# A two-block transformer kernel at 256 tokens: index scores over 128 rows, the start reordered, the final norm split, tensors moved by 64 bytes

## The chip, the cores and the metric

The kernel runs on one core of a Trainium2 chip. The metric is device time in microseconds (us), lower is better. TensorE (PE) multiplies; its weight loads (PEld) overlap its matmuls. VectorE (DVE), ScalarE (ACT), GpSimd (POOL) and SyncE (SP) are the other engines; SP issues nearly all transfers.

## The reference

`x` is 256 rows of 2048, all in float32. Two layers of a first block (an attention with index scores, then a block attention), one layer of a second block (a gated delta net beside a compressed attention, then a gated feed-forward of width 5632), and a last norm. What matters for the change:

```python
# layer a: index scores
qi = rope(qi.reshape(B, T, IDX_HEADS, IDX_DIM), pos)      # 16 heads of 64
ki = rope(ki.reshape(B, T, 1, IDX_DIM), pos)[:, :, 0]     # one key of 64
rel = relu(einsum('bqhd,bsd->bqhs', qib, ki) * IDX_DIM ** -0.5)
score = einsum('bqh,bqhs->bqs', wib, rel)
_, sel = lax.top_k(score, n_keep)                          # 64 of 256 keys
...
# the feed-forward, and the final norm
x = x + (silu(h2 @ w_ffn_gate) * (h2 @ w_ffn_up)) @ w_ffn_down
return x * lax.rsqrt(mean(x * x, axis=-1) + NORM_EPS) * norm_f_w
```

## The kernel before

Every product with weights runs in "chunks" of 512 output columns (`weight_plan`). A chunk is a row of "quads": a quad is 4 x 128 rows of the weight (1 MB), landed in one of four buffers `W`. Float32 is split into a rounded high part and a rest: ScalarE writes `WH` (`round_up`), VectorE the rest `WL` (`rest`, L1673), each in two halves of 128x1024, and TensorE adds three matmuls, WH with XH, WL with XH, WH with XL (L795, L796, L797), each 128x128 times 128x512. The activations stand turned, as XH and XL; for the last product of the feed-forward they are HH and HL. A half quad is two "visits", one for each 128 rows of x, of six matmuls each. The sums stand in two banks ACC, which ScalarE or VectorE empties at the end of a chunk (`take`).

All other work (norms, attention, delta net, turning x) is written as generators, started at a fixed visit by `side_plan` on every engine and advanced one step at each visit (`sides_of`). So each engine's order is fixed by program order, and semaphores join them. TensorE's side steps thus lie between two groups of six main matmuls.

The places of the change:

- Start. `turn("x.a", c)` turns slice c (512 columns) of x: TensorE transposes four 128x128 tiles into bank TP0 and four into TP1 (L428), ScalarE writes XH with the norm's gain (L818, two of 128x256 for each bank), VectorE XL (L1198, L1199). Slices 0 and 1 are turned ahead of the loop over the chunks; 2 and 3 are side tasks at visits 2 and 6. In the prologue ScalarE and VectorE do for n = 0 and 1: the whole of slice n, then both halves of quad n's weights. SP issues slice, quad, slice, quad in turn (L386, L399).
- ScalarE's helper `A` loads a table before Exp or Ln if another is held (L814); another load is put at L818 where an activation needs one. The roots of the first norm are taken at visit 11; `take` of the first chunk scales by them.
- Index scores (`index` on three engines). After rotation VectorE copies the one key of 64 twice, side by side, into KI (L1337, L1338), so that its transpose KIT holds the key in partitions 0 to 63 and again in 64 to 127. QIT holds two heads above each other. For head h TensorE multiplies the 64 partitions of its half, in two matmuls (L525, L526) of 128 and 256 columns, one head a visit; ScalarE takes relu, VectorE adds it into SCORE (L1354), and then, in eight rounds of `max` and `match_replace`, finds the 64 largest. The attention's scores have the same two shapes over 128 partitions (L464, L465).
- Addresses. Tensors are laid one after another. `root_steps` has 100 columns; behind it come the arena (all scratch), SG, H, HH, HL and the final gain.
- End. Squares of each slice of the last x are summed by ScalarE (`squares("f", c)`), slices 0 to 2 as side tasks in the last chunks, slice 3 after the loop. `roots` takes the mean, Ln, Exp and one refinement on VectorE. Then VectorE scales each 128 rows of 2048 by root and gain in one pass (L1703), and SP stores them (L403).

```python
    for n in range(2):                       # act_program; dve_program alike, with rest
        for _ in turn("x.a", n):
            pass
        for half in range(2):
            round_up(n, half)
...
    for t in range(TB):                      # dve_program, its end
        STT(M.X[:, t, :], M.X[:, t, :], M.rs[:, 4, t:t + 1], M.NF, ALU.mult, ALU.mult).then_inc(*did("normalised", t))
```

## Time and profile before

| | before |
|---|---|
| median of 3 runs | 2363.6 us (2363.17 to 2369.43) |
| the profiled execution | 2363.92 us, of which the span 2362.6 |
| TensorE matmuls busy | 2322.3 us, 98% of the span |
| VectorE busy | 1367.0 us, 58% |
| ScalarE busy | 1158.6 us, 49% |
| mean granted TensorE clock | 0.997 |
| read from HBM | 396.23 MB, 169 GB/s over the span |

The span runs from the first to the last instruction of the profiled execution; its own time is 1.3 us more. The busy share of TensorE is of the instructions as recorded, which overlap: a main matmul lasts 0.39 us, and the next starts 0.23 us after it. So its speed is read from starts.

### The profile page before, as it was taken

The numbers are of one execution on the slowest core, as the hardware profiler recorded it, in microseconds if no ns is written. First come the engines' busy times: TensorE is split into PE (matmuls) and PEld (weight loads), VectorE is DVE, ScalarE is ACT, GpSimd is POOL, SyncE is SP. The second block draws the span as 40 slices with busy tenths as digits, with TensorE's granted clock in tenths as the row PEclk, the third lists the DMA queues.
The fourth block names the chain that finished last, engine by engine and source line by source line (L and its number), as shares of the span: only waits on it lengthen the run. The fifth ranks groups of instructions, "written<-read, shape, count | busy, mean of one in ns | idle before, by whom it ended". The sixth has DMA issues, their size and how long they took to land.

```text
span 2362.6 us, 27386 instructions
## 1 busy us (share of the span) xinstructions
PE 2322.3 (98%) x11188; PEld 1921.5 (81%) x11188; DVE 1367.0 (58%) x1930; ACT 1158.6 (49%) x1635; POOL 9.6 (0%) x17
## 2 busy tenths in 40 slices
PE   8999999999999999999999999999999999999997
PEld 6788788888788888888888887888888888888886
DVE  5676555656555577687666555645545544544554
ACT  5456654556654564453445455445444344434443
POOL 0000000000000000000000000000000000000000
PEclk9999999999999999999999999999999999999999
DMA  7454445564545553333554455555565565555552
GB/s 260 132 177 153 143 154 188 174 196 143 162 159 196 161 166 107 125 126 107 166 191 143 157 164 178 178 196 193 181 195 181 194 192 184 194 184 191 195 179 107
DMA packets 204269, 400.10 MB, mean 169 GB/s; under 512 B 12656, under 2 KB 12816, under 8 KB 203760
## 3 DMA queue, kind: packets, MB, share of 16 engines
q1 hardware_dynamic: 201920, 391.08, 50.3%
q0 software_dynamic: 1648, 6.32, 1.0%
q8 instruction: 89, 1.46, 0.3%
q10 hardware_dynamic: 576, 0.95, 0.1%
q14 instruction: 36, 0.29, 0.0%
HBM read 396.23 MB, written 2.10 MB: 169 GB/s over the span
## 4 chain that ended last, share of the span: by engine, by line
PE 93%; DVE 3%; ACT 2%; issue 1%; DMA 0%; SPq 0%; DVEq 0%; ACTq 0%
PE ACC L795 28%; PE ACC L797 27%; PE ACC L796 27%; PE TP L428 2%; ACT arena L818 1%; PE PV L629 1%; PE SC L624 1%; DVE WL L1673 1%; PE PV L632 1%; PE SC L465 1%; PE TP L473 1%; PE SC L675 1%; PE PV L483 0%; PE PV L482 0%; PE PV L481 0%
## 5 line engine op out<-in xcount | busy, mean ns | idle before, releaser
L1673 DVE TENSOR_TENSOR WL<-W,WH 128x1024 fp32r<-128x1024 f32 x740 | 900.8, 1219 | 656.0 <-ACT WH L818 654.3
L818 ACT ACTIVATE WH<-W 128x1024 fp32r<-128x1024 f32 x740 | 781.3, 1056 | 839.6 <-PE ACC L797 835.3
L795 PE MATMUL ACC<-WH,XH 128*128 128x512 f32 x2592 | 1045.7, 403 | 7.0 <-ACT arena L818 4.8
L797 PE MATMUL ACC<-WH,XL 128*128 128x512 f32 x2592 | 1013.5, 391 | 0.0
L796 PE MATMUL ACC<-WL,XH 128*128 128x512 f32 x2592 | 1011.7, 390 | 0.0
L795 PEld LDWEIGHTS ACC<-WH,XH 128*128 128x128 f32 x2592 | 488.1, 188 | 116.8 <-issue 15.2
L797 PEld LDWEIGHTS ACC<-WH,XL 128*128 128x128 f32 x2592 | 487.4, 188 | 105.9
L796 PEld LDWEIGHTS ACC<-WL,XH 128*128 128x128 f32 x2592 | 488.7, 189 | 92.1 <-issue 1.0
L795 PE MATMUL ACC<-WH,HH 128*128 128x512 f32 x352 | 139.3, 396 | 0.0
L797 PE MATMUL ACC<-WH,HL 128*128 128x512 f32 x352 | 137.8, 392 | 0.0
L796 PE MATMUL ACC<-WL,HH 128*128 128x512 f32 x352 | 137.6, 391 | 0.0
L818 ACT ACTIVATE arena<-ACC,reciprocal_roots 128x512 f32<-128x512 f32 x86 | 58.9, 688 | 44.3 <-PE ACC L797 44.0
L795 PEld LDWEIGHTS ACC<-WH,HH 128*128 128x128 f32 x352 | 66.1, 188 | 16.6 <-DVE X L1667 1.8
L797 PEld LDWEIGHTS ACC<-WH,HL 128*128 128x128 f32 x352 | 66.1, 188 | 14.9
L796 PEld LDWEIGHTS ACC<-WL,HH 128*128 128x128 f32 x352 | 66.2, 188 | 13.7
L818 ACT ACTIVATE arena<-SC 128x256 f32<-128x256 f32 (+2 forms) x70 | 27.1, 391 | 90.8 <-PE SC L624 65.1
L818 ACT ACTIVATE arena<-TP 128x384 f32<-128x384 f32 (+2 forms) x91 | 46.2, 510 | 42.4 <-PE TP L473 21.6
L1667 DVE TENSOR_TENSOR X<-ACC,X 128x512 f32<-128x512 f32 x48 | 33.0, 687 | 43.7 <-PE ACC L797 43.7
L818 ACT ACTIVATE arena<-arena,maxima 128x128 f32<-128x128 f32 x96 | 42.6, 446 | 15.0 <-DVE maxima L1299 14.9
L1196 DVE TENSOR_TENSOR XL<-TP,XH 128x512 fp32r<-128x512 f32 x32 | 22.1, 691 | 38.5 <-ACT XH L818 38.5
L818 ACT ACTIVATE arena<-arena 128x512 f32<-128x512 f32 (+4 forms) x50 | 37.0, 756 | 12.2 <-DVE arena L1419 9.6
L1511 DVE TENSOR_TENSOR arena<-arena,PV 128x256 f32<-128x256 f32 x48 | 20.2, 421 | 34.2 <-PE PV L632 23.0
(255 smaller groups left out, 1414.2 us busy)
## 6 DMA issues: line engine op xcount, KB each, us to landing
W<-in_w_in SPq DMA_DIRECT2D x84, 1024.0 KB, 4.9
W<-in_a_w_in SPq DMA_DIRECT2D x48, 1024.0 KB, 5.1
W<-in_w_ffn_gate SPq DMA_DIRECT2D x44, 1024.0 KB, 5.2
W<-in_w_ffn_up SPq DMA_DIRECT2D x44, 1024.0 KB, 5.2
W<-in_w_ffn_down SPq DMA_DIRECT2D x44, 1024.0 KB, 5.1
W<-in_b_w_in SPq DMA_DIRECT2D x40, 1024.0 KB, 5.1
W<-in_a_w_out SPq DMA_DIRECT2D x16, 1024.0 KB, 5.0
W<-in_b_w_out SPq DMA_DIRECT2D x16, 1024.0 KB, 5.1
```

The source lines that it names most:

```text
L428: ins = TR(TP[j][:, (2 * k + t) * P:(2 * k + t + 1) * P], src(c)[:, t, col:col + P], ident)
L465: MM(SC[b][:, P:3 * P], QT[:, i, P:T], kt(0, T), start=True, stop=True).then_inc(*did("scores_multiplied", l, g, i))
L473: ins = TR(TP[b][:, s * P:(s + 1) * P], M_PR(l)[b][:, s * P:(s + 1) * P], ident)
L624: ins = MM(sc[:, h * P:(h + 1) * P], m["M"][:, h, :], m["S"][:, h, :], start=True, stop=True)
L629: ins = MM(pv[:, h * P:(h + 1) * P], m["TI"][:, h, :], m["Y"][:, h, :], start=True, stop=True)
L632: ins = MM(pv[:, (PH + h) * P:(PH + h + 1) * P], m["Y"][:, h, :], m["TI"][:, h, :], start=True, stop=True)
L795: MM(out, hx, WH[:, k, 0:ch.width], start=q == 0 and k == 0, stop=False)
L796: MM(out, hx, WL[:, k, 0:ch.width], start=False, stop=False)
L797: ins = MM(out, lx, WH[:, k, 0:ch.width], start=False, stop=last and k == QK - 1)
L818: return nc.scalar.activation(out, in_, func, **how)
L1667: ins = TT(x, acc, x, ALU.add)
L1673: TT(tiles_of(M.WL[n % 2], ch, half), tiles_of(M.W[n % 4], ch, half), tiles_of(M.WH[n % 2], ch, half).bitcast(F32), ALU.subtract).then_inc ...
```

## The change

Five things, all in one edit:

1. KI and KIT become two of each: one holds the key in partitions 0 to 63 and zeros above, the other zeros and the key. Head h multiplies all 128 partitions of QIT, which hold two heads, with the KIT that has zeros for the other head. Both are placed elsewhere in the arena.
2. Of slice 1 of x, TensorE's transposes move into the loop, as a side task at visits 0 and 1. ScalarE and VectorE alternate in the prologue: half a slice, half a quad.
3. The table for Ln and Exp is loaded at ScalarE's start, and for the final norm ahead of the squares of slice 0.
4. Slices 0 to 2 of the last x are multiplied by the final gain as side tasks (`gained`), three visits after each is ready. The scaling by the root is shared: ScalarE takes the left 1024 columns and stores them from its own queue, VectorE the right 1024 (the last 512 with their gain), stored by SP.
5. `root_steps` gets 116 columns, which moves all that lies behind it by 64 bytes: arena, SG, H, HH, HL and the final gain began 64 bytes past a multiple of 128, and now begin on one.

```diff
+    begin(0, "second_turn")
     for c in range(2, NC_D):
         begin(4 * c - 6, "turn", "x.a", c)
...
         begin(after(f"d.p2c{c}"), "squares", "f", c)
+        begin(after(f"d.p2c{c}") + 3, "gained", c)
...
-    M.dn_norms, roots = sb("delta_norms", [P, 2, 8]), sb("root_steps", [P, 100])
+    M.dn_norms, roots = sb("delta_norms", [P, 2, 8]), sb("root_steps", [P, 116])
...
-    M.KW, M.KI, M.WI, M.KIT, M.TOP = cut(18944, TB, ID + IH), cut(19104, TB, 2 * ID), cut(19360, TB, IH), cut(19392, T), cut(19648, TB, 8)
+    M.KW, M.KI, M.WI, M.KIT, M.TOP = cut(18944, TB, ID + IH), cut(21200, TB, 2, 2 * ID), cut(19360, TB, IH), cut(21712, 2, T), cut(19648, TB, 8)
...
-        sp.dma_start(K.out[0, t * P:(t + 1) * P, :], M.X[:, t, :]).then_inc(*did("x_stored", t, by=16))
+        sp.dma_start(K.out[0, t * P:(t + 1) * P, 2 * CH:], M.X[:, t, 2 * CH:]).then_inc(*did("x_stored", t, by=16))
...
+    sp.wait_ge(*at("x_stored_left", TB - 1))
...
-        for t in range(TB):
-            ins = TR(TP[0][:, t * P:(t + 1) * P], M.KI[:, t, :], ident)
+        for odd in range(2):
+            for t in range(TB):
+                ins = TR(TP[0][:, (odd * TB + t) * P:(odd * TB + t + 1) * P], M.KI[:, t, odd, :], ident)
...
-            MM(banks[b][:, 0:P], M.QIT[half, h // 2, 0:P], M.KIT[half, 0:P], start=True, stop=True)
-            MM(banks[b][:, P:3 * P], M.QIT[half, h // 2, P:T], M.KIT[half, :], start=True, stop=True).then_inc(*did("index_scored", h))
+            MM(banks[b][:, 0:P], M.QIT[:, h // 2, 0:P], M.KIT[:, h % 2, 0:P], start=True, stop=True)
+            MM(banks[b][:, P:3 * P], M.QIT[:, h // 2, P:T], M.KIT[:, h % 2, :], start=True, stop=True).then_inc(*did("index_scored", h))
...
-    for c in range(2):
-        for _ in turn("x.a", c):
-            pass
+    for _ in turn("x.a", 0):
+        pass
+
+    def second_turn():
+        yield from turn("x.a", 1)
...
+        if l == "f" and c == 0:
+            act.preload_act_table_set("natural_log_exp_and_others")
+            held[0] = "log_exp"
...
+    act.preload_act_table_set("natural_log_exp_and_others")
+    held[0] = "log_exp"
     act.wait_ge(*at("gains_landed"))
     for n in range(2):
-        for _ in turn("x.a", n):
-            pass
-        for half in range(2):
+        for half, _ in enumerate(turn("x.a", n)):
             round_up(n, half)
...
+    act.wait_ge(*at("gained", 1))
+    act.wait_ge(*at("reciprocal_roots", "f"))
+    for t in range(TB):
+        x = M.X[:, t, 0:2 * CH]
+        A(x, x, ACT.Copy, scale=M.rs[:, 4, t:t + 1]).then_inc(*did("normalised_left", t))
+        act.wait_ge(*at("normalised_left", t))
+        act.dma_start(K.out[0, t * P:(t + 1) * P, 0:2 * CH], x).then_inc(*did("x_stored_left", t, by=16))
...
-        V.tensor_copy(M.KI[:, :, 0:ID], M.KW[:, :, 0:ID])
-        V.tensor_copy(M.KI[:, :, ID:2 * ID], M.KW[:, :, 0:ID])
+        for odd in range(2):
+            V.tensor_copy(M.KI[:, :, odd, odd * ID:(odd + 1) * ID], M.KW[:, :, 0:ID])
+            V.memset(M.KI[:, :, odd, (1 - odd) * ID:(2 - odd) * ID], 0.0)
...
+    def gained(c):
+
+        dve.wait_ge(*at("final_gain_landed"))
+        dve.wait_ge(*at("squares_summed", "f", c))
+        x = M.X[:, :, c * CH:(c + 1) * CH]
+        TT(x, x, M.NF[:, c * CH:(c + 1) * CH].unsqueeze(1).to_broadcast([P, TB, CH]), ALU.mult).then_inc(*did("gained", c))
+        yield
...
-        STT(M.X[:, t, :], M.X[:, t, :], M.rs[:, 4, t:t + 1], M.NF, ALU.mult, ALU.mult).then_inc(*did("normalised", t))
+        x, y = (M.X[:, t, c * CH:(c + 1) * CH] for c in (2, 3))
+        STT(y, y, M.rs[:, 4, t:t + 1], M.NF[:, 3 * CH:], ALU.mult, ALU.mult)
+        TS(x, x, M.rs[:, 4, t:t + 1], None, ALU.mult).then_inc(*did("normalised", t))
```

How instructions move, at three places. ScalarE at the start, before: a table load, the whole slice, then both halves of the quad.

```order
L1154 DMA gains<-in_norm_gains 128x64
L818 ACT_TABLE_LOAD
L818 ACTIVATE XH<-TP,gains 128x256 x4
L818 ACTIVATE WH<-W 128x1024 x2
L818 ACTIVATE XH<-TP,gains 128x256 x4
L818 ACTIVATE WH<-W 128x1024 x2
```

And now (lines are shifted by the edit, L818 is L825):

```order
L1164 DMA gains<-in_norm_gains 128x64
L1165 ACT_TABLE_LOAD
L825 ACTIVATE XH<-TP,gains 128x256 x2
L825 ACTIVATE WH<-W 128x1024
L825 ACTIVATE XH<-TP,gains 128x256 x2
L825 ACTIVATE WH<-W 128x1024
```

The first rounding of weights moved ahead of the second half of the slice, and the load of the table no longer follows a wait for a transpose.

TensorE at the start, before (16 transposes, then the main matmuls):

```order
L428 MATMUL TP<-consts,X 128x128 x16
L795 MATMUL ACC<-WH,XH 128x512
L796 MATMUL ACC<-WL,XH 128x512
L797 MATMUL ACC<-WH,XL 128x512
L795 MATMUL ACC<-WH,XH 128x512
```

And now (L428 is L431, L795 to L797 are L802 to L804):

```order
L431 MATMUL TP<-consts,X 128x128 x8
L802 MATMUL ACC<-WH,XH 128x512
L803 MATMUL ACC<-WL,XH 128x512
L804 MATMUL ACC<-WH,XL 128x512
L802 MATMUL ACC<-WH,XH 128x512
L803 MATMUL ACC<-WL,XH 128x512
L804 MATMUL ACC<-WH,XL 128x512
L431 MATMUL TP<-consts,X 128x128 x4
```

Eight transposes, those of slice 1, moved behind the first and (the other four) the second six main matmuls.

VectorE at the end, before:

```order
L1667 TENSOR_TENSOR X<-ACC,X 128x512 x2
L1207 TENSOR_REDUCE root_steps<-sums_of_squares 128x2
L1209 TENSOR_SCALAR root_steps<-root_steps 128x2
L1231 TENSOR_TENSOR root_steps<-reciprocal_roots 128x2
L1233 SCALAR_TENSOR_TENSOR root_steps<-root_steps 128x2
L1235 SCALAR_TENSOR_TENSOR reciprocal_roots<-root_steps,reciprocal_roots 128x2
L1703 SCALAR_TENSOR_TENSOR X<-X,reciprocal_roots,final_gain 128x2048 x2
```

And now, where L1672 is the gain of one slice, done between the roundings of the last weights:

```order
L1672 TENSOR_TENSOR X<-X,final_gain 128x2x512
L1700 TENSOR_TENSOR WL<-W,WH 128x1024
L1694 TENSOR_TENSOR X<-ACC,X 128x512 x2
L1224 TENSOR_REDUCE root_steps<-sums_of_squares 128x2
L1226 TENSOR_SCALAR root_steps<-root_steps 128x2
L1248 TENSOR_TENSOR root_steps<-reciprocal_roots 128x2
L1250 SCALAR_TENSOR_TENSOR root_steps<-root_steps 128x2
L1252 SCALAR_TENSOR_TENSOR reciprocal_roots<-root_steps,reciprocal_roots 128x2
L1729 SCALAR_TENSOR_TENSOR X<-X,reciprocal_roots,final_gain 128x512
L1730 TENSOR_SCALAR X<-X,reciprocal_roots 128x512
L1729 SCALAR_TENSOR_TENSOR X<-X,reciprocal_roots,final_gain 128x512
L1730 TENSOR_SCALAR X<-X,reciprocal_roots 128x512
```

Of the two passes of 2048 columns behind the roots, four of 512 are left on VectorE.

## Rows read from the trace of the kernel before

**Rows 1.** The page, part 4: chain that ended last, by engine
```profile
PE 93%; DVE 3%; ACT 2%; issue 1%; DMA 0%; SPq 0%; DVEq 0%; ACTq 0%
```
**Rows 2.** Timeline of the start: start us, us, engine, line, operation, [idle before <-releaser]
```profile
1.23 0.48 SPq L399 DMA_DIRECT2D W<-in_a_w_in  x1
...
5.54 1.94 PE L428 MATMUL TP<-consts,X 128*128 128x128 f32 x8 [5.54 <-DMA X<-in_x]
6.71 1.28 ACT L818 ACT_TABLE_LOAD   x1 [6.71 <-PE TP L428]
...
9.45 2.02 ACT L818 ACTIVATE WH<-W 128x1024 fp32r<-128x1024 f32 x2
...
11.83 0.79 PE L795 MATMUL ACC<-WH,XH 128*128 128x512 f32 x1
...
14.98 0.56 PE L796 MATMUL ACC<-WL,XH 128*128 128x512 f32 x1
```
**Rows 3.** The transfer issued at 1.23: KB, us from issue to landing
```profile
W<-in_a_w_in SPq DMA_DIRECT2D x1, 1024.0 KB, 7.2
```
**Rows 4.** Timeline of the end of the first chunk
```profile
34.98 1.28 ACT L814 ACT_TABLE_LOAD   x1 [0.52 <-DVE root_steps L1209]
...
38.51 1.25 ACT L818 ACTIVATE arena<-ACC,reciprocal_roots 128x512 f32<-128x512 f32 x2
...
39.32 0.47 PE L795 MATMUL ACC<-WH,XH 128*128 128x512 f32 x1 [1.91 <-ACT arena L818]
```
**Rows 5.** Timeline, TensorE around one index score
```profile
83.31 0.40 PE L797 MATMUL ACC<-WH,XL 128*128 128x512 f32 x1
...
83.64 0.29 PEld L525 LDWEIGHTS SC<-arena 64*128 64x128 f32 x2 [0.36 <-issue]
...
84.49 0.19 PEld L795 LDWEIGHTS ACC<-WH,XH 128*128 128x128 f32 x1 [0.33 <-issue]
```
**Rows 6.** Timeline, TensorE around one score of the attention
```profile
168.16 0.39 PE L797 MATMUL ACC<-WH,XL 128*128 128x512 f32 x1
...
168.85 0.58 PE L795 MATMUL ACC<-WH,XH 128*128 128x512 f32 x1
```
**Rows 7.** Timeline ahead of the first index transpose
```profile
74.13 0.18 DVE L1339 TENSOR_SCALAR arena<-arena 128x32 f32<-128x32 f32 x1
...
74.39 0.59 PEld L509 LDWEIGHTS TP<-consts,arena 128*128 128x128 f32 x4
```
**Rows 8.** Windows: us, busy (x instructions) of PE, PEld, DVE, ACT, POOL, clock, DMA, GB/s
```profile
102.20:121.70 19.50, 19.50 (x84) 12.59 (x83) 16.72 (x30) 8.93 (x15) 0.00 (x0) 1.00 0.33 108
122.00:145.00 23.00, 23.00 (x104) 18.82 (x104) 22.52 (x62) 10.63 (x12) 0.00 (x0) 1.00 0.46 145
```
**Rows 9.** Timeline, TensorE's wait behind the choice of the largest
```profile
139.78 0.19 PEld L795 LDWEIGHTS ACC<-WH,XH 128*128 128x128 f32 x1 [0.29 <-DVE WL L1673]
```
**Rows 10.** Timeline, first and last of 179 matmuls with XH, of 65 with HH
```profile
1708.30 0.39 PE L796 MATMUL ACC<-WL,XH 128*128 128x512 f32 x1
...
1748.67 0.39 PE L797 MATMUL ACC<-WH,XL 128*128 128x512 f32 x1
...
2334.33 0.40 PE L796 MATMUL ACC<-WL,HH 128*128 128x512 f32 x1
...
2348.99 0.39 PE L797 MATMUL ACC<-WH,HL 128*128 128x512 f32 x1
```
**Rows 11.** Windows of these two stretches
```profile
2334.30:2349.00 14.70, 14.70 (x66) 12.02 (x64) 4.05 (x4) 3.16 (x7) 0.00 (x0) 1.00 0.01 1
1708.30:1748.70 40.40, 40.40 (x180) 33.41 (x178) 19.98 (x18) 17.64 (x18) 0.00 (x0) 1.00 0.61 195
```
**Rows 12.** Timeline of the end
```profile
2351.39 1.28 ACT L814 ACT_TABLE_LOAD   x1 [0.52 <-DVE root_steps L1209]
...
2353.82 4.61 DVE L1703 SCALAR_TENSOR_TENSOR X<-X,reciprocal_roots,final_gain 128x2048 f32<-128x2048 f32 x2
2356.20 2.62 SPq L403 DMA_DIRECT2D out<-X  x2
```

More of the change, by code:

```diff
@@ L521, in index @@
         for h in range(IH):
-            b, half = h % 4, slice(ID * (h % 2), ID * (h % 2 + 1))
+            b = h % 4
             name = ("SC0", "SC1", "PV0", "PV1")[b]
             wait_empty(name)
-            MM(banks[b][:, 0:P], M.QIT[half, h // 2, 0:P], M.KIT[half, 0:P], start=True, stop=True)
-            MM(banks[b][:, P:3 * P], M.QIT[half, h // 2, P:T], M.KIT[half, :], start=True, stop=True).then_inc(*did("index_scored", h))
+            MM(banks[b][:, 0:P], M.QIT[:, h // 2, 0:P], M.KIT[:, h % 2, 0:P], start=True, stop=True)
+            MM(banks[b][:, P:3 * P], M.QIT[:, h // 2, P:T], M.KIT[:, h % 2, :], start=True, stop=True).then_inc(*did("index_scored", h))
             emptied[name] = ("index_taken", h)
@@ L758, in narrow @@
         yield
-    tasks["narrow"] = narrow
+    tasks["narrow"], tasks["second_turn"] = narrow, second_turn
     live, visit, taken = [], 0, [None] * TB
@@ L925, in index @@
         act.wait_ge(*at("index_transposed", 4))
-        A(M.KIT, TP[0][:, 0:T], ACT.Copy).then_inc(*did("index_turned", 4))
+        A(M.KIT.rearrange("p n t -> p (n t)"), TP[0][:, :], ACT.Copy).then_inc(*did("index_turned", 4))
         yield
@@ L1676, in dve_program @@
                  dn_gates=dn_gates, dn_conv=dn_conv, dn_norms=dn_norms, dn=dn, dn_out=dn_out, nsa_rope=nsa_rope, compress=compress, compressed=compressed,
-                 nsa_queries=nsa_queries, nsa_attend=nsa_attend, mixed=mixed)
+                 nsa_queries=nsa_queries, nsa_attend=nsa_attend, mixed=mixed, gained=gained)
     dve.wait_ge(*at("gains_landed"))
     for n in range(2):
-        for _ in turn("x.a", n):
-            pass
-        for half in range(2):
+        for half, _ in enumerate(turn("x.a", n)):
             rest(n, half)
@@ L1699, in dve_program @@
         pass
-    dve.wait_ge(*at("final_gain_landed"))
+    dve.wait_ge(*at("gained", 2))
     dve.wait_ge(*at("reciprocal_roots", "f"))
     for t in range(TB):
-        STT(M.X[:, t, :], M.X[:, t, :], M.rs[:, 4, t:t + 1], M.NF, ALU.mult, ALU.mult).then_inc(*did("normalised", t))
+        x, y = (M.X[:, t, c * CH:(c + 1) * CH] for c in (2, 3))
+        STT(y, y, M.rs[:, 4, t:t + 1], M.NF[:, 3 * CH:], ALU.mult, ALU.mult)
+        TS(x, x, M.rs[:, 4, t:t + 1], None, ALU.mult).then_inc(*did("normalised", t))
 def pool_program(K):
```

## The prediction

> **What bounds the kernel.** I read first the chain of waits: 93% of it is TensorE's own work [rows 1]. So what the change saves on TensorE, or where TensorE stands still, is saved in full; work taken from the other engines is worth nothing unless TensorE, or the end, waits for it. Then, in this order: the start and the end instruction by instruction, where TensorE is not yet, or no longer, the bound; the stretch of the index scores, for what lies between two main matmuls; then the steady pace of the matmuls by operand.
>
> About 0.3% (7.1 us) is what a measurement of this kernel can tell from no change.
>
> **The start.** TensorE turns slice 0 at 5.54, and ScalarE, woken by it, first loads a table (6.71 to 7.99), then writes four XH pieces and rounds the first weights from 9.45; 2.38 us later, at 11.83, the first weight matmul starts [rows 2]. The weights themselves were issued at 1.23 [rows 2] and took 7.2 us [rows 3]: they were there at 8.43. In the new order the table is loaded before any wait (1.28 us gone) and the first rounding stands behind two XH pieces instead of four; the four pieces fill 7.99 to 9.45, 0.37 each, so two are done near 7.5 and the rounding starts when the weights land, 8.43. That moves TensorE's start by 9.45 - 8.43 = 1.0 earlier, to 10.8.
> Against it: the eight transposes of slice 1 stood ahead of that matmul, while TensorE had nothing else; now four follow each of the first two groups of six matmuls. Eight take 1.94 [rows 2] at the lower clock (1.2 GHz, which is what a matmul start every 0.45 from 11.83 to 14.98 is, eight starts, seven intervals [rows 2]; steady it is 0.227, below). If all eight run at the low level, TensorE is 1.94 - 1.0 = 0.9 behind; if the second four come after the rise, they cost half and it is 0.5 behind; if the rise follows the earlier start, it is even. I take 0.3 behind, ends -1.0 and +0.9.
> At the end of the first product TensorE stands idle for 1.91, until 39.32, while ScalarE empties the accumulator (from 38.51). In ScalarE's unbroken work ahead of that is a table load at 34.98 of 1.28 [rows 4], which is gone: the table from the start serves Ln and Exp too. So 38.51 - 1.28 + 0.3 = 37.53, and with the same 0.81 from emptying to matmul TensorE goes on at 38.34: **-1.0**. TensorE itself is free at 39.32 - 1.91 + 0.3 = 37.7, so ScalarE still decides. Ends: -2.3 and -0.4.
>
> **The index scores.** There are 16 visits, each with products of 128 and of 256 columns over 64 rows between two groups of main matmuls. From the start of the last main matmul to that of the next, 83.31 to 84.49, is 1.18, with two holes in weight loading that nothing explains, 0.36 and 0.33, at the change to the 64-row form and back [rows 5]. A product of the same columns over 128 rows, the scores of the attention, takes 168.16 to 168.85 = 0.69 [rows 6], with no hole. The new scores have just this form: 16 x 0.49 = **-7.8**. The zeros cost no column. Two more transposes of the key: at 1.94 / 8 at the low clock, half of that at the high, +0.2. VectorE clears two half blocks more ahead of the first index transpose; its last small step there takes 0.18 and ends at 74.31, and TensorE's weight load starts at 74.39 [rows 7]; so of two such steps, overlapping a little, some 0.3, 0.2 shows: **+0.2**. ScalarE's copy of 512 instead of 256 columns lies behind six main matmuls (1.4 us).
> What is late next is VectorE. From its first step for one score to that for the eighth after it (102.2 to 121.7) it is busy 16.72 of 19.50 us, 2.8 free [rows 8]; eight shorter visits take away 8 x 0.49 = 3.9. It falls at least 1.1 behind; since it must still idle a little at the first of them I take 1.4. Behind it comes the choice of the largest 64, in which it is busy 22.52 of 23.0 [rows 8], and at 139.78 TensorE already waits 0.29 for VectorE's WL [rows 9]. So nothing of the lag is made up before that wait, and it comes out as **+1.4** there. Ends: 0 (later work has slack) and +3.9 (all of those eight visits).
>
> **The operand at 128 bytes.** Sixteen more columns in the table of root steps move the arena, SG, H, HH and HL by 64 bytes, from 64 beyond a multiple of 128 to a multiple; X, XH, XL and the weights already lie on one. In two stretches without side work the matmuls with XH take (1748.67 - 1708.30) / 178 = 0.2268, those with HH (2348.99 - 2334.33) / 64 = 0.2291 [rows 10]. Other work is not what slows HH: in its stretch 1 GB/s is moved and VectorE and ScalarE are nearly idle, in that of XH 195 GB/s [rows 11]. There are 1,056 HH or HL matmuls: 1,056 x 0.0023 = **-2.4**, if the address is the reason; the only other difference is which tensor. Ends: -2.4 and 0. The attention's products read the arena but are paced by their passes, so I give them nothing.
>
> **The end.** After the last square, ScalarE loads a table (2351.39, 1.28), VectorE starts scaling at 2353.82, and SyncE issues the first store at 2356.20, 2.38 later; the last byte is in 6.4 after that, at 2362.6 [rows 12]. The table is now loaded ahead of the final squares of slice 0, where ScalarE only waits for TensorE: -1.28. The gain is multiplied in ahead, after each of three slices, 1.2 us of VectorE while it idles between roundings. What stays is, per 128 rows, 512 + 512 columns on VectorE and 1024 on ScalarE, side by side. A 1024-column pass of ScalarE takes 1.0 (the pair of roundings at 9.45 takes 2.02) [rows 2] and VectorE's two passes at most half of the 2.3 of 2048 columns (4.61 for two) [rows 12], so the first stores go out about 1.1 after the start of scaling instead of 2.38: -1.27. The same 2.1 MB then leave in the same 6.4, as second stores follow 1.1 to 1.6 later, well before the first are out. Sum **-2.5**; ends -1.3 (store no earlier) and -3.2.
> The Trainium skill (ScalarE: Activation LUTs, What ACT_TABLE_LOAD costs) adds a drain of 1.38 us to every load; by it the two loads on the path would give 2.8 more and the kernel 2348.9. Here such a drain finds no room: from the last load's end, 2352.67, to the scaling at 2353.82 are 1.15, and Ln, Exp and three steps of VectorE lie in them. The trace bears out the 1.28 alone.
>
> **Sum.** -1.0 - 7.8 + 0.2 + 0.2 + 1.4 - 2.4 - 2.5 = -11.9. The profiled execution took 2363.92 for a span of 2362.6; its time becomes 2352.0. The median of the runs shown is 0.3 lower, so I predict **2351.7**.
>
> **Rivals.**
> (a) The address is not why HH is slower (its data, or its being written by another path). All else holds: 2354.1. For it: no row compares one tensor at two addresses. Against it: XH and HH have the same shape and writers.
> (b) VectorE keeps more: the full 3.9. Then 2354.2. For it: 22.52 of 23.0 busy. Against: VectorE's own 2.8 free in that stretch.
> (c) The padded scores do not do what they say: the holes belong to the alternation of these two shapes, not to 64 rows. Then -7.8 and +1.4 both go: 2358.1, no change by the bound. Against it: [rows 6] alternates the same two shapes in the same place without a hole.
> (d) A load holds ScalarE longer than its row: the idle 0.52 ahead of the one at 34.98, put down to VectorE, is the load's own, and so at the end. Then 1.0 more goes: 2350.7. Against it: both stand right behind a step of VectorE that Ln needs anyway. (The Trainium skill's drain, above, would be the larger form of this.)
> (e) Slower: TensorE's clock. The change leaves TensorE idle from 7.5 to 10.8 and then mixes short transposes into the first matmuls. Each microsecond longer at 1.2 GHz costs 1 - 0.227 / 0.45 = 0.5. It takes 24 us more at the low level to use up the 11.9, and about 38 to be 0.3% slower, 2371. For it: [rows 2] shows the low level at this place. Against it: there it was over within 3.5 us of steady matmuls.
> Each stall that is moved may also gain or lose such a stretch, at 0.5 per microsecond 1 to 2 us either way.
>
> **Chances.** Forecast 0.64, own range 2349 to 2355; (a) 0.12; (b) 0.08; (c) 0.07; (d) 0.04; (e) 0.02; several small ones failing together, near 2357, 0.03. Faster by over 0.3% (below 2356.5) are the forecast, (a), (b) and (d): 0.88. Within: (c) and the last, 0.10. Slower: 0.02. The range for 8 in 10 takes in (a), (b), (d) and the ends of the unknown costs: 2347.5 to 2357.0.
>
> **What would show it.** Right: 0.69 between the main matmuls around each score, no hole; HH's pace 0.2268; one table load fewer ahead of 40 us and none after the last matmul; the first store 4.7 us after the start of the last matmul, where it is 2356.20 - 2348.99 = 7.2 now; TensorE waiting 1.5 us on WL shortly after the index stretch, where it now waits 0.3. Wrong, and with it the number: visits still near 1.18; HH still 0.2291; a longer stretch of the low clock at the start; a wait for the stores' second halves.

## The result, and the profile after

The changed kernel takes 2352.48 us, median of five runs (2351.88 to 2353.9), against 2363.6 for five runs of the kernel before (2360.28 to 2369.82): a ratio of 0.9937, 95% interval 0.9916 to 0.9959. Predicted were 2351.7 and faster. The profiled execution took 2353.76 for a span of 2352.4; its prediction was 2352.0.

| | after |
|---|---|
| span of the profiled execution | 2352.4 us (-10.2) |
| TensorE matmuls busy | 2313.6 us, 98% |
| VectorE, ScalarE busy | 1368.8, 1159.8 us |
| mean granted TensorE clock | 0.997 |

The page's chain of waits says the same as [rows 1]:

```profile
PE 92%; DVE 4%; ACT 2%; issue 1%; DMA 0%; ACTq 0%; SPq 0%; DVEq 0%
```

The busy sums tell nothing of where 10 us went. What tells it is the start of each of the 8,832 main matmuls, which stand in the same order in both kernels. The table sets before and after side by side, numbered from 0.

| main matmul | before | after | difference | what lies in between |
|---|---|---|---|---|
| 0 | 11.83 | 10.57 | -1.26 | the start |
| 24 | 19.87 | 20.31 | +0.44 | eight transposes in the loop |
| 96 | 39.32 | 38.47 | -0.85 | no table load ahead of the first emptying |
| 246 | 82.08 | 81.40 | -0.68 | two more key transposes, +0.22 |
| 342 | 121.50 | 114.45 | -7.05 | 16 index scores, -6.37 |
| 420 | 139.78 | 133.80 | -5.98 | the wait for WL, +1.07 |
| 6432 | 1792.32 | 1786.21 | -6.11 | nothing that stays: no single place moves it by more than 0.4 |
| 8831, the last | 2348.99 | 2341.09 | -7.90 | HH, -1.8 |
| end of the span | 2362.6 | 2352.4 | -10.2 | the end, -2.3 |

Both profiles hold the same two short stretches at a granted clock of 0.50, 3.4 us each (from 264.5 and 1165.6 before, from 258.1 and 1159.2 after), so this table sets like beside like.

The start, in the timeline of the changed kernel, which answers to [rows 2]:

```profile
1.74 1.28 ACT L1165 ACT_TABLE_LOAD   x1 [1.74 <-issue]
...
6.78 0.84 ACT L825 ACTIVATE XH<-TP,gains 128x256 fp32r<-128x256 f32 x2 [3.75 <-DMA gains<-in_norm_gains]
...
8.21 1.06 ACT L825 ACTIVATE WH<-W 128x1024 fp32r<-128x1024 f32 x1 [0.58 <-DMA W<-in_a_w_in]
...
9.29 1.22 DVE L1700 TENSOR_TENSOR WL<-W,WH 128x1024 fp32r<-128x1024 f32 x1 [0.69 <-ACT WH L825]
...
10.57 0.80 PE L802 MATMUL ACC<-WH,XH 128*128 128x512 f32 x1 [3.18 <-DVE WL L1700]
```

The table is in before anything is waited for, and ScalarE then waits 0.58 for the weights: the rounding cannot start earlier than 8.21, as predicted (8.43). The first matmul is released by VectorE's WL. The end of the first chunk, which answers to [rows 4]:

```profile
35.42 0.20 ACT L825 ACTIVATE reciprocal_roots<-root_steps 128x2 f32<-128x2 f32 x1 [0.53 <-DVE root_steps L1226]
...
37.66 1.24 ACT L825 ACTIVATE arena<-ACC,reciprocal_roots 128x512 f32<-128x512 f32 x2
...
38.47 0.47 PE L802 MATMUL ACC<-WH,XH 128*128 128x512 f32 x1 [0.63 <-ACT arena L825]
```

TensorE's idle time went from 1.91 to 0.63. The 0.53 ahead of the root stays although no load follows it: it was never the load's. One index score, in the timeline of TensorE:

```profile
84.68 0.40 PE L804 MATMUL ACC<-WH,XL 128*128 128x512 f32 x1
84.91 0.38 PE L529 MATMUL SC<-arena 128*128 128x128 f32 x2
85.13 0.60 PE L530 MATMUL SC<-arena 128*128 128x256 f32 x2
85.38 0.58 PE L802 MATMUL ACC<-WH,XH 128*128 128x512 f32 x1
85.79 0.39 PE L803 MATMUL ACC<-WL,XH 128*128 128x512 f32 x1
```

From main to main it is 0.70, as the attention's [rows 6], and no weight load waits. But look one matmul further: 85.38 to 85.79 is 0.41. In the kernel before, behind the hole, it is less:

```profile
84.49 0.50 PE L795 MATMUL ACC<-WH,XH 128*128 128x512 f32 x1
84.82 0.39 PE L796 MATMUL ACC<-WL,XH 128*128 128x512 f32 x1
```

That is 0.33. So from the last main matmul ahead of the score to the second one behind it, a score takes from 83.31 to 84.82 = 1.51 before and 84.68 to 85.79 = 1.11 now: 0.40, not 0.49. Then the wait for the weights' low parts, which answers to [rows 9]:

```profile
132.53 1.22 DVE L1700 TENSOR_TENSOR WL<-W,WH 128x1024 fp32r<-128x1024 f32 x1
...
133.79 0.19 PEld L802 LDWEIGHTS ACC<-WH,XH 128*128 128x128 f32 x1 [1.29 <-DVE WL L1700]
133.80 0.50 PE L802 MATMUL ACC<-WH,XH 128*128 128x512 f32 x1 [0.87 <-DVE WL L1700]
```

An undisturbed stretch with HH, first and last of 65, which answers to [rows 10]:

```profile
2326.56 0.40 PE L803 MATMUL ACC<-WL,HH 128*128 128x512 f32 x1
...
2341.09 0.39 PE L804 MATMUL ACC<-WH,HL 128*128 128x512 f32 x1
```

14.53 for 64 intervals is 0.2270 each (before 0.2291). And the end, which answers to [rows 12]:

```profile
2343.50 0.20 ACT L825 ACTIVATE reciprocal_roots<-root_steps 128x2 f32<-128x2 f32 x1 [0.54 <-DVE root_steps L1226]
...
2344.62 1.15 ACT L825 ACTIVATE X<-X,reciprocal_roots 128x1024 f32<-128x1024 f32 x1 [0.68 <-DVE reciprocal_roots L1252]
2344.64 0.75 DVE L1729 SCALAR_TENSOR_TENSOR X<-X,reciprocal_roots,final_gain 128x512 f32<-128x512 f32 x1
2345.31 0.48 DVE L1730 TENSOR_SCALAR X<-X,reciprocal_roots 128x512 f32<-128x512 f32 x1
...
2345.80 0.37 ACTq L1197 DMA_DIRECT2D out<-X  x1
2345.82 1.42 SPq L405 DMA_DIRECT2D out<-X  x2
```

No table load; ScalarE and VectorE are done within 0.02 of each other, and the first store is issued 4.71 after the last matmul's start (before 7.2).

### The profile page after: what moved, and what is told of

It reads as the page before. It is cut to its first block, busy times and chain, and to the rows that moved or that the text cites. A ratio compares the mean times of both kernels' runs of the same rounds, so it can differ in the third digit from the quotient of the medians.

```text
span 2352.4 us, 27404 instructions
## 1 busy us (share of the span) xinstructions
PE 2313.6 (98%) x11190; PEld 1923.8 (82%) x11190; DVE 1368.8 (58%) x1937; ACT 1159.8 (49%) x1636; POOL 9.6 (0%) x17
## 4 chain that ended last, share of the span: by engine, by line
PE 92%; DVE 4%; ACT 2%; issue 1%; DMA 0%; ACTq 0%; SPq 0%; DVEq 0%
PE ACC L802 27%; PE ACC L804 27%; PE ACC L803 27%; PE TP L431 2%; ACT arena L825 1%; DVE WL L1700 1%; PE PV L633 1%; PE SC L628 1%; PE PV L636 1%; PE SC L468 1%; PE TP L476 1%; PE SC L679 1%; PE PV L485 0%; PE PV L486 0%; PE PV L484 0%
## 5 line engine op out<-in xcount | busy, mean ns | idle before, releaser
L825 ACT ACTIVATE WH<-W 128x1024 fp32r<-128x1024 f32 x740 | 781.4, 1056 | 835.8 <-PE ACC L804 832.8
L802 PE MATMUL ACC<-WH,XH 128*128 128x512 f32 x2592 | 1046.9, 404 | 9.8 <-DVE WL L1700 4.0
L804 PE MATMUL ACC<-WH,XL 128*128 128x512 f32 x2592 | 1013.5, 391 | 0.0
L802 PEld LDWEIGHTS ACC<-WH,XH 128*128 128x128 f32 x2592 | 488.4, 188 | 115.0 <-issue 9.0
L804 PEld LDWEIGHTS ACC<-WH,XL 128*128 128x128 f32 x2592 | 487.2, 188 | 105.2
L802 PE MATMUL ACC<-WH,HH 128*128 128x512 f32 x352 | 138.6, 394 | 0.0
L804 PE MATMUL ACC<-WH,HL 128*128 128x512 f32 x352 | 137.1, 389 | 0.0
L825 ACT ACTIVATE arena<-ACC,reciprocal_roots 128x512 f32<-128x512 f32 x86 | 58.9, 689 | 44.1 <-PE ACC L804 43.8
L802 PEld LDWEIGHTS ACC<-WH,HH 128*128 128x128 f32 x352 | 66.1, 188 | 16.5 <-DVE X L1694 2.0
L804 PEld LDWEIGHTS ACC<-WH,HL 128*128 128x128 f32 x352 | 66.1, 188 | 14.0
L825 ACT ACTIVATE arena<-SC 128x256 f32<-128x256 f32 (+2 forms) x70 | 27.1, 390 | 88.2 <-PE SC L628 65.4
L825 ACT ACTIVATE arena<-TP 128x384 f32<-128x384 f32 (+2 forms) x91 | 46.4, 513 | 42.6 <-PE TP L476 21.4
L825 ACT ACTIVATE arena<-arena,maxima 128x128 f32<-128x128 f32 x96 | 42.7, 447 | 15.0 <-DVE maxima L1316 14.9
L825 ACT ACTIVATE arena<-arena 128x512 f32<-128x512 f32 (+4 forms) x50 | 37.1, 756 | 12.2 <-DVE arena L1438 9.7
L825 ACT ACTIVATE XH<-TP,gains 128x256 fp32r<-128x256 f32 x64 | 26.8, 470 | 27.1 <-PE TP L431 23.3
```

The costliest lines, as they stand in the source:

```text
L802: MM(out, hx, WH[:, k, 0:ch.width], start=q == 0 and k == 0, stop=False)
L804: ins = MM(out, lx, WH[:, k, 0:ch.width], start=False, stop=last and k == QK - 1)
L825: return nc.scalar.activation(out, in_, func, **how)
```

## The experiments

Twelve kernels, each built from the one before or the changed one.

### The operand's address: the shift alone, and each operand by itself

Of the two operands of a main matmul the expectations call the 128x128 of activations (XH, XL, HH, HL) the stationary one and the 128x512 of weights (WH, WL) the moving one. `shift_only` is the kernel before with `root_steps` at 116 columns, nothing else. The other three move one operand:

```diff
-    M.dn_norms, roots = sb("delta_norms", [P, 2, 8]), sb("root_steps", [P, 100])      # shift_only
+    M.dn_norms, roots = sb("delta_norms", [P, 2, 8]), sb("root_steps", [P, 116])
...
+    sb("gap_ahead_of_hh", [P, 16])      # hh_only: HH, HL at 0 mod 128, the arena still at 64
...
+    sb("gap_ahead_of_xh", [P, 16])      # xh_64: XH, XL at 64 mod 128; a gap behind them restores the rest
...
+    sb("gap_ahead_of_wh", [P, 16])      # wh_64: WH, WL at 64 mod 128; a gap behind them restores the rest
```

> The kernel before, with root_steps of 116 columns: arena, SG, H, HH, HL and the gain all move from 64 off to a multiple of 128. Theory: HH's pace 0.2269, 2.3 us less, and the arena's products are paced by their passes and keep their times (an attention score 0.69 between main matmuls, the delta net's eight products 1.05): 2361.3. Rival (the arena's stationary operands gain too): those groups get shorter by 2 ns for each product and the time falls 2 to 4 us further.

> The kernel before, with 64 bytes of unused columns ahead of HH: HH, HL and the final gain lie on multiples of 128 bytes, arena, SG and H stay 64 off. Theory (the address of the stationary operand sets the pace): the 1,056 matmuls with HH go from one every 0.2291 us to one every 0.2269, 2.3 us in all, and nothing else moves. Rival (a) (HH's data or its writers): the pace stays 0.2291 and the time at 2363.6. A third reading, that the arena or H must move too, also leaves 0.2291.

> The kernel before, with 64 bytes of unused columns ahead of XH and 64 more behind XL: only XH and XL are moved, to 64 bytes past a multiple of 128. Theory (address of the stationary operand): the 7,776 main matmuls with XH slow from 0.2269 to 0.2291, so 7,776 x 0.0022 = 17 us, less what hides in waits: about 2380. Rival (a) (it is something of HH as a tensor): XH keeps 0.2269 and the time 2363.6.

> The kernel before, with WH and WL alone moved to 64 bytes past a multiple of 128: the moving operand of all 8,832 main matmuls. Theory in its narrow form (only the stationary operand's address counts): both paces as before, 0.2269 with XH and 0.2291 with HH, time 2363.6. Rival in its wide form (any operand off 128 bytes costs): both 0.0022 slower, 19 us, about 2383.

Measured: `shift_only` 2359.57 us, `hh_only` 2369.68, `xh_64` 2383.85, `wh_64` 2373.53, the kernel before in the same job 2372.65. These totals are one run each and carry something else (below, the clock: its mean was 0.997 in `shift_only` and `wh_64`, 0.992 or 0.993 in the others), so the pace is what counts. `shift_only`, for one, is 1.7 under the 2361.3 expected because its profile has no stretch at 0.50 near 1165 us. Timeline of `wh_64`, first and last of 191 matmuls with XH and of 65 with HH:

```profile
1891.49 0.39 PE L798 MATMUL ACC<-WL,XH 128*128 128x512 f32 x1
...
1934.98 0.39 PE L799 MATMUL ACC<-WH,XL 128*128 128x512 f32 x1
...
2344.11 0.39 PE L798 MATMUL ACC<-WL,HH 128*128 128x512 f32 x1
...
2358.62 0.39 PE L799 MATMUL ACC<-WH,HL 128*128 128x512 f32 x1
```

43.49 / 190 = 0.2289 with XH, which stands on a multiple of 128; 14.51 / 64 = 0.2267 with HH, which does not, and nor do the weights. With XH at 64 and the weights at 0 (`xh_64`) XH too is slow, 190 intervals of 0.2290:

```profile
1900.73 0.40 PE L798 MATMUL ACC<-WL,XH 128*128 128x512 f32 x1
...
1944.24 0.39 PE L799 MATMUL ACC<-WH,XL 128*128 128x512 f32 x1
```

So what decides is neither operand's own alignment, but whether both begin at the same place within 128 bytes. My expectation of `wh_64` had no such case. Over all undisturbed stretches, in ns:

| weights mod 128 | activations mod 128 | start to start | kernels |
|---|---|---|---|
| 0 | 0 | 226.9 | XH in all but two; HH after, `hh_only`, `shift_only` |
| 0 | 64 | 229.0 | HH before; XH and HH in `xh_64` |
| 64 | 0 | 229.1 | XH in `wh_64` |
| 64 | 64 | 227.0 | HH in `wh_64` |
| 0 | 32 | 233.3 | HH in `hh_32` |

`hh_only` and `shift_only` have the same pace. In `shift_only`, which moves the arena too, no interval with attention or delta net work in it, of some 450 up to matmul 3900, changed by more than 0.07 us, and all of them together by 0.3: the arena's move gains next to nothing.

`hh_32` is the changed kernel with `root_steps` at 124 columns, so HH begins 32 past a multiple of 128.

> The changed kernel, with root_steps of 124 columns instead of 116: all behind it, HH among it, lies 32 bytes past a multiple of 128. Theory A (the operand must start on a multiple of 128): HH's pace is 0.2291 or slower again, 2.3 us more than the changed kernel. Theory B (multiples of 32 are enough except 64): 0.2269 and no difference. The index scores and the end keep their times in both.

```profile
2333.56 0.40 PE L803 MATMUL ACC<-WL,HH 128*128 128x512 f32 x1
...
2348.49 0.40 PE L804 MATMUL ACC<-WH,HL 128*128 128x512 f32 x1
```

14.93 / 64 = 0.2333 here and over all stretches; all HH matmuls together take 5.75 us more than in the changed kernel, and the run took 2361.14. A quarter of 128 bytes off costs more than a half.

### The start and the end, each alone

`turn_only`: the kernel before with the second slice's transposes in the loop and half-and-half prologues. `table_only`: with the early load alone. `end_only`: with part 4 and the load ahead of the last squares.

```diff
+    act.preload_act_table_set("natural_log_exp_and_others")      # table_only: these two lines
+    held[0] = "log_exp"
...
-        for _ in turn("x.a", n):                                  # turn_only: this and second_turn
-            pass
-        for half in range(2):
+        for half, _ in enumerate(turn("x.a", n)):
...
+        begin(after(f"d.p2c{c}") + 3, "gained", c)                # end_only: this, gained and the shared scaling
```

> The kernel before, with slice 1 turned behind the first weights (all three engines' orders of the start as in the changed kernel) but the tables loaded where they were. Theory: the first main matmul starts near 10.9 to 11.6 instead of 11.83 (the table load of 1.28 still stands ahead of XH, so the weights' rounding starts at 8.73, not 8.43), the 25th some 0.4 to 0.8 us later than before (19.87), because eight transposes now run in the stream, and the 97th at 39.32 + 0.4 to 0.8, since the table load at 35 us is still in ScalarE's chain: about 0.5 us slower than before. Rival (the turning order itself gains): the 97th starts before 39.32.

> The kernel before, with only the table for Ln and Exp loaded at ScalarE's start. Theory: the four XH pieces start at 6.7 instead of 8.0 and the weights' rounding at 8.43, so the first main matmul starts no later than the transposes of slice 1 end, near 11.9 (they wait for slice 1, which lands at 9.9): no gain there; the gain is at the 97th main matmul, 39.32 - 1.28 + 0, bounded by the emptying of the accumulator behind TensorE: 38.1. So 1.2 us less than before, all of it from the second table load. Rival (the reordered turning is what gains at the start): less than 0.5 us.

> The kernel before, with only the end changed: gain ahead, scaling and stores shared, and the table loaded ahead of the final squares. Theory: up to the last matmul nothing moves (within 0.2 us); first store 4.7 us after the last matmul's start instead of 7.2, end 11.3 after it instead of 13.6: 2.3 us less. Rival (work put into the last chunks on VectorE and ScalarE delays the last weights): the last matmul starts more than 0.3 us later than 2348.99.

Measured: `turn_only` 2374.27 us, `table_only` 2361.71, the kernel before in the same job 2363.06, one run each. The total of `turn_only` carries some 10 us of the clock (below), so the starts are compared. "Rise" is where the pace of the main matmuls doubles, from one every 0.43 us to one every 0.23; the last column is matmul 96 less half of the rise.

| | matmul 0 | matmul 24 | matmul 96 | rise | matmul 96, less half the rise |
|---|---|---|---|---|---|
| before | 11.83 | 19.87 | 39.32 | 15.3 | 31.7 |
| `turn_only` | 11.07 | 20.70 | 40.13 | 16.1 | 32.1 |
| `table_only` | 11.46 | 19.89 | 38.06 | 15.9 | 30.1 |
| after | 10.57 | 20.31 | 38.47 | 15.8 | 30.6 |

The early table gives -1.26 at matmul 96. The new order of turning gives an earlier first matmul and then loses it: +0.8 alone, +0.4 beside the early table. But the rise moves from kernel to kernel without a cause in the code: among the eight kernels whose start is that of the kernel before it lies between 13.8 and 16.0, and matmul 96 between 38.52 and 39.58. Each microsecond at half pace costs half a microsecond. With half of the rise taken off, these eight agree within 0.1 (31.6 to 31.7), so the last column is the one to compare: the order costs 0.4 alone and 0.5 beside the early table, the table gives -1.6, and the whole start -1.1. `table_only` in the timeline:

```profile
38.06 0.47 PE L795 MATMUL ACC<-WH,XH 128*128 128x512 f32 x1 [0.63 <-ACT arena L818]
```

`end_only` took 2360.49 (before, same job, 2363.06). From the last main matmul's start, 2347.83, to the end of its span, 2359.1, it is 11.3, where it was 13.6: -2.3.

### The scores: the part alone, and two heads at once

`index_only` is the kernel before with part 1 alone:

```diff
-            MM(banks[b][:, 0:P], M.QIT[half, h // 2, 0:P], M.KIT[half, 0:P], start=True, stop=True)
+            MM(banks[b][:, 0:P], M.QIT[:, h // 2, 0:P], M.KIT[:, h % 2, 0:P], start=True, stop=True)
```

> The kernel before with the scores over 128 rows alone (the two copies of the keys with zeros, and their transposes). Rows of the changed kernel: a visit of scores that puts two 64-row matmuls ahead of a main matmul held the main stream for 2.44 us from one main matmul to the second one after it, and one of 128 rows holds it for 2.035, so 0.405 each. My theory, corrected by that: 16 visits give -6.5, the two more key transposes +0.2, and VectorE, which comes to its next three-term products earlier against the same keys' work, makes TensorE wait about 1 us longer near 134 us: -5.3 in all, and nothing outside 74 to 141 us: a step that stays to the end, and about 0.9977 of the time before. The prediction as it stood (0.49 a visit, +0.4, +1.4) says -6.0 here. The rival, that the holes belong to the alternation of the small matmuls with the main ones and not to the 64 rows, says no step in the stretch of scores: -0 or slower by the wait.

Measured: 2359.44 us, median of 12; the ratio to the kernel before is 0.9972 (0.9957 to 0.9988), where its runs spread from 2359.88 to 2373.97. By starts: from matmul 246 to 342 -6.2 for the 16 visits, key transposes +0.22, a wait for WL at matmul 420 with a step of +0.95. From 96 on that is -5.0 at matmul 420, against -5.3 expected, and nothing of the edit comes later: the further -1.2 by matmul 1000 is the stretch at 0.50 that the kernel before has at 264.5 and this profile lacks. The ratio of the totals, 6.6 us, says more than the edit gives, since the kernel before spent more of its runs at the lower clock (below); at a mean granted clock of 0.997 in both, it is 2357.7 to 2357.8 against 2362.6 to 2364.4. The rival of alternation falls: there was no visit that kept its holes.

`two_heads` keeps the 64-row scores of the kernel before, but puts two heads in every other gap:

```diff
             emptied[name] = ("index_taken", h)
-            yield
+            if h % 2:
+                yield
+                yield
```

> The kernel before, with its 64-row scores, but two heads (four small matmuls) at every other gap between main matmuls instead of one head at each. If the holes belong to the change between a 128-row and a 64-row form (my theory), there are 8 pairs of them instead of 16: two heads hold the main stream for little more than one visit's holes (0.36 and 0.33 us) once, and the stretch of scores shortens by 8 x 0.4 = 3.2 us. If a hole belongs to each 64-row matmul, or to the step from the lower half of the rows to the upper (the two heads of a visit use one each), nothing is won, or holes appear between the two heads of a visit. The 128-row matmuls of the changed kernel would be right by either of them, so this run tells only what the price is paid for.

Measured: 2358.03 us, and from matmul 246 to 342 -8.3, more than the changed kernel's -6.4 and far more than the 3.2 expected. One visit in the timeline of TensorE:

```profile
88.98 0.39 PE L799 MATMUL ACC<-WH,XL 128*128 128x512 f32 x1
89.30 0.50 PE L525 MATMUL PV<-arena 64*128 64x128 f32 x4
89.62 0.61 PE L526 MATMUL PV<-arena 64*128 64x256 f32 x4
90.16 0.50 PE L797 MATMUL ACC<-WH,XH 128*128 128x512 f32 x1
90.50 0.39 PE L798 MATMUL ACC<-WL,XH 128*128 128x512 f32 x1
```

Two heads take 88.98 to 90.50 = 1.52 here, one head 1.51 before. The reason is in the starts. The timeline up to 89.33 already holds two records, one of each head:

```profile
89.30 0.39 PE L525 MATMUL PV<-arena 64*128 64x128 f32 x2
```

The heads use the two halves of the rows, and run side by side. So my count was right in one thing, the holes are paid at the change of form and once for both heads, and missed another, that the second head then costs nothing. The Trainium skill (TensorEngine Tiling (Array Packing), Key Properties) has both: changing the tiling mode drains TensorE, and different tiles run in parallel. It gives no price; here the change there and back costs 0.4 more than two 128-row matmuls in the same place, and a pair of heads 1.52 against 2 x 1.11. Part of the gain is lost again: VectorE falls further behind, and TensorE waits for WL at matmul 408 (an interval of 0.95) as well as at 420 (1.26). From 246 to 420 -6.4 is left, where the changed kernel has -5.3. The run's total holds, beside this, 1.6 us of a stretch at 0.50 from 39.9 that the kernel before's profile doesn't have.

### Where VectorE's lag comes from, and two edits together

`keys_later` is the changed kernel with the attention's key norm and turn begun 20 visits later (the expectation says matmuls; it is groups of six):

```diff
-        begin(after(l + ".k"), "keys", l)
+        begin(after(l + ".k") + (20 if l == "a" else 0), "keys", l)
```

> The changed kernel with the norm and turn of the attention's keys begun 20 matmuls later, so that VectorE chooses the largest scores first. In the changed kernel TensorE waits 0.87 us near 133.8 us for VectorE's low parts of WL, a step of +1.0 us against the kernel before. My theory: VectorE is late there because the keys' work stands ahead of the choice; with it behind, the three-term products are met in time, the wait goes, and the time falls by 1.0 us (0.9996 of the changed kernel's), with nothing new late, since the keys are wanted first by the attention's scores after 150 us. The rival: VectorE's total work up to 140 us decides, whatever its order, and the same wait comes back at the same place or one product later: no change. A second rival: keys that come later hold the attention's first scores, +1 or more.

Measured: 2356.38 us, median of 12, 0.9959 of the kernel before (0.9943 to 0.9974). My theory fell and both rivals held. The step at matmul 420 is still there, +1.01, and the keys came too late, so that the interval at matmul 462 is 3.15 us, in the timeline:

```profile
144.56 0.66 PE L445 MATMUL TP<-consts,arena 128*128 128x128 f32 x4 [2.36 <-DVE arena L1265]
```

VectorE did idle again before the choice, but the two groups of key transposes (0.9 us of TensorE's intervals) had left the stretch too, so TensorE reached the wait that much earlier. By matmul 700, counted from matmul 96, `keys_later` is 2.7 us behind the changed kernel. The timeline of VectorE in the changed kernel shows what the wait really follows: one half of weights behind the other, with two rounds of the choice between,

```profile
120.87 1.22 DVE L1700 TENSOR_TENSOR WL<-W,WH 128x1024 fp32r<-128x1024 f32 x1
...
124.75 1.22 DVE L1700 TENSOR_TENSOR WL<-W,WH 128x1024 fp32r<-128x1024 f32 x1
...
128.64 1.22 DVE L1700 TENSOR_TENSOR WL<-W,WH 128x1024 fp32r<-128x1024 f32 x1
```

one each 3.88, while TensorE uses one each 2.72 (12 x 0.227). That is the same 3.88 in the kernel before, whose TensorE arrives later and waits 0.29. So once it has begun, the choice makes WL late whatever stands ahead of it. One round at every other visit would need 2.6 per half (an estimate: 3.88 less one round of 1.3) and fit; it was not tried.

`best` is `keys_later` with both slices turned ahead of the first weights, as before.

> The changed kernel with two edits: the attention's keys begun 20 matmuls later, and both slices of X turned ahead of the first weights, as before (the table of logarithm and exponential is still loaded ahead, the arena still moved, scores over 128 rows, split end). By the runs so far the other order of turning costs about 0.8 us in the first chunk (97th main matmul at 40.13 against 39.32 without the early table; 38.47 against 38.06 with it, so 0.4 there), and the wait for the low parts of WL 1.0. My theory: 0.4 + 1.0 = 1.4 us less than the changed kernel, about 0.9994 of it. The rival: what is won at the start is lost again at the first wait for a slice of weights from memory, and only the 1.0 or nothing stays.

Measured: 2355.23 us, median of 9, 0.9954 of the kernel before (0.9935 to 0.9972). The changed kernel's own 0.9937 (0.9916 to 0.9959) is from another chip, and the intervals overlap: no version is shown to beat it. Against `keys_later` beside it, 2356.38, the medians differ by 1.15. Matmul 96 came at 36.25 instead of 37.92, but the rise came at 12.4 instead of 14.4; less half the rise it is 30.1 against 30.7, so the order of turning is worth 0.6. As in `keys_later`, the interval at matmul 462 is 3.2 us, for the late keys; its profiled execution, 2351.13, is fast because it has no stretch at 0.50 at all, where `keys_later` and the changed kernel have two of 3.4 us.

## Why the prediction was right, and its terms wrong by

- **Bound.** Every gain on TensorE came through in full: the differences add up along the main matmuls and nothing gave them back. Right.
- **The start, -1.0.** Measured -0.85 in this pair of profiles, -1.1 with the rise at the same time. The table's -1.26 was in the prediction as 1.28; the +0.3 for the transposes is +0.4. Of its three cases the middle one came: four transposes at the low level, four after the rise, 0.5 behind by the prediction and 0.44 at matmul 24. The first matmul came 1.26 earlier against 1.0. The rise itself came 0.5 later in the kernel's time, which no step of the prediction could say. Right in each step, also in ScalarE deciding.
- **Index scores, -7.8.** Measured -6.4, the largest miss. The step that failed is the reading of one interval only: 1.18 against 0.69, last main matmul to next. The second interval after was not read, and there the 64-row form gets back 0.08 (0.33 against 0.41). The mechanism, a price for the change of form that 128 rows do not pay, was right; `index_only` has it alone with the same size.
- **Key transposes, +0.2.** Measured +0.22.
- **VectorE's clearing, +0.2.** Measured 0: the transposes of the index queries begin at the same distance from matmul 96 as before.
- **VectorE's lag, +1.4.** Measured +1.07. The place was right, and the wait was sized by VectorE's free time; with visits that save 0.40 instead of 0.49 the lag is 8 x 0.40 - 2.8 = 0.4 at least, and the measured 1.07 is 0.7 above that floor, where I had added 0.3 to mine. TensorE's interval there is 1.26 instead of 0.26.
- **HH, -2.4.** Measured -1.8. The pace came out as said, 0.227. The saving per matmul was taken as 0.0023 against XH's pace; in the undisturbed stretch it is (14.66 - 14.53) / 64 = 0.0020, and next to side work less. One reading was loose: in [rows 11] VectorE and ScalarE are not nearly idle beside HH but busy 4.05 and 3.16 of 14.70 us, about half of their share beside XH. The reason given, that HH began off a multiple of 128, is only half of it: it is the distance to the weights within 128 bytes.
- **The end, -2.5.** Measured -2.3: the stores are all in 6.6 after the first issue (2345.80 to 2352.4) instead of 6.4.
- **Sum.** Predicted -11.9, measured -10.2 between the profiled executions. The 1.4 of the scores and 0.6 of HH are partly paid back by the lag and the clearing. That the median is nearer, 2352.48 against 2351.7, is luck: it lies 1.3 below the profiled execution, where 0.3 was taken.
- **Rivals.** (a) fell by `hh_only` and `shift_only`; (b) by the step at matmul 420; (c) by `index_only`; (d) by the 0.53 and 0.54 that stay without a load, in the two stretches above, and by `table_only`, where the load gone gives 1.26, or 1.6 with the rise at the same time. (e): no run of the changed kernel was slower, though the low level did last 1.7 us longer at the start (10.6 to 15.8 instead of 11.8 to 15.3), 0.9 us by the prediction's own 0.5 per microsecond; it is inside the -0.85. The Trainium skill (ScalarE: Activation LUTs, What ACT_TABLE_LOAD costs) puts a drain of 1.38 us beside each load; by it the load gone ahead of matmul 96 had to give 2.66, and these runs do not bear it out.

## What to carry to other kernels

Read a hole in TensorE's stream up to the second matmul behind it, since a pipelined neighbour takes part of it back. Place the two operands of the most frequent matmul at the same offset within 128 bytes; it costs nothing and was worth 1% of the pace here. Before padding 64-row products to 128, try two of them side by side in the two halves: one change of form, and the second product free. Here it left 6.4 us from matmul 246 to 420 where padding left 5.3, and it needs no second copy of the key. When two profiles are compared by starts, look first where the clock stood at 0.50 in each: here it moved single places by up to 1.7 us, and whole runs by 10. And give an engine's long side task a step that fits beside its regular work, or the regular work is late wherever the task is placed.

## What the runs showed of the hardware

**The relative address**, in the table above: 226.9 ns with equal offsets, 229.0 at 64 apart, 233.3 with the activations 32 behind a multiple of 128 and the weights on one. No other distance was tried.

**The clock in the middle.** TensorE waits about 2 us at a time for VectorE in the compression stage, and in some executions the granted clock then falls. In `turn_only` (2374.27 us), behind such a wait (timeline, then windows: us, PE busy, granted clock, DMA share, GB/s):

```profile
1163.83 1.94 PE L676 MATMUL SC<-arena 128*128 128x30 f32 x16 [1.96 <-DVE arena L1569]
```

```profile
1173.00:1175.00 2.00, 2.00 (x6) 0.50 0.00 0
1178.00:1181.00 3.00, 3.00 (x9) 0.50 0.00 0
```

and in the kernel before, same stage:

```profile
1171.00:1175.00 4.00, 4.00 (x27) 1.00 0.00 0
1178.00:1181.00 3.00, 3.00 (x15) 1.00 0.37 74
```

0.50 is the lower level, 1.2 GHz. In the clock records of the traces it lasts 23.9 us from 1166.4 in `turn_only` and as long in `xh_64`, 20.5 in `hh_only`, 3.4 from 1165.6 in the kernel before and 3.4 in the changed one (from 1159.2); `shift_only`, `wh_64` and `best` have none there. Between 1150 and 1200 us `turn_only` loses 9.6 us and `hh_only` 8.0 to the kernel before, and `shift_only` gains 1.7. That accounts for what `turn_only` and `hh_only` took beyond their edits. The kernel before, in the last job's 26 runs, is near 2360, 2363 or 2369 to 2374, in 16 of them the last, while 12 runs of `index_only` stay under 2362.1. The mean granted clock, on record for each, goes with the group: 0.998 in the four near 2360, 0.997 in the six from 2362.6 to 2364.4, 0.992 to 0.994 in the sixteen. So it is the clock in all of them; that it is lost in this stretch is read from the profiled runs and argued for the others. The changed kernel does not avoid the stretch, since its own profile has the short form of it. Whether it avoids the long form or its five runs (0.997 and 0.998) were lucky isn't settled: of the 21 runs of `keys_later` and `best`, 5 lie some 9 us above the rest, at 0.993 or 0.994.

**The start.** The first main matmuls start every 0.43 us, at half the steady pace, as in the stretch at 0.50 above. I took that for the lower clock level. The windows seem to speak against it, since they print a granted clock of 1.00 there (changed kernel):

```profile
0.00:5.00 5.00, 0.00 (x0) 1.00 0.53 155
11.00:15.40 4.40, 4.40 (x13) 1.00 1.05 389
```

But they print the same 1.00 for the first 5 us, in which TensorE had run nothing. The trace has no clock record that early: in thirteen of the fourteen traces the first record, of 1.00, begins within 0.2 us of where the pace doubles (in `hh_32`, whose first record is at 16.7, side work stands at that place). Six of them:

| | first clock record | first interval of 0.23 begins |
|---|---|---|
| `best` | 12.39 | 12.47 |
| `end_only` | 13.78 | 13.87 |
| `keys_later` | 14.43 | 14.59 |
| before | 15.32 | 15.38 |
| after | 15.78 | 15.83 |
| `table_only` | 15.90 | 15.87 |

So the printed 1.00 ahead of the record says nothing, and the pace and the record together bear the prediction's reading out: TensorE starts at the lower level and is granted the full clock at the rise. When that comes differs without cause in the code, by 2.2 us among the eight kernels with the start of the kernel before.
